# Eight heads at once in the top-16 look-up of a two-block model: bf16 look-up, pair sums for four heads, and gate groups behind 50 units

## What is computed

```python
q = (xt @ wq).reshape(T, PEER_HEADS, 2, PEER_DQ_HALF)
s1 = jnp.einsum('thd,nd->thn', q[:, :, 0], k1)      # 8 heads, 128 sub-keys
s2 = jnp.einsum('thd,nd->thn', q[:, :, 1], k2)
v1, i1 = lax.top_k(s1, 16)
v2, i2 = lax.top_k(s2, 16)
cand = (v1[..., :, None] + v2[..., None, :]).reshape(T, 8, 256)
cidx = (i1[..., :, None] * 128 + i2[..., None, :]).reshape(T, 8, 256)
sc, pos = lax.top_k(cand, 16)
eidx = jnp.take_along_axis(cidx, pos, axis=-1)
gate = jax.nn.softmax(sc, axis=-1)
# per token: sum over its 128 experts e of gate_e * gelu(x . u_e) * v_e
```

## Time and profile before

| | us |
|---|---|
| median of 3 runs | 3374.56 (3369.22 to 3378.02) |
| the profiled execution, its own time | 3360.43 |
| span of its trace | 3358.7 |
| PE busy | 3090.0 (92%) |
| DVE busy | 2289.5 (68%) |
| ACT busy | 1543.4 (46%) |
| mean granted TensorE clock | 0.957 |

### The profile page before, as it was taken

How to read it: one execution, slowest core, us unless ns; L and a number is a source line. 1 busy time by engine, 2 the same in 40 slices (tenths; PEclk the granted TensorE clock), 3 DMA queues, 4 the chain that set the end, 5 groups by cost and what they waited for, 6 DMA issues and landing times.

```text
span 3358.7 us, 59174 instructions
## 1 busy us (share of the span) xinstructions
PE 3090.0 (92%) x20832; PEld 2821.1 (84%) x20832; DVE 2289.5 (68%) x4056; ACT 1543.4 (46%) x2322; POOL 145.0 (4%) x135
## 2 busy tenths in 40 slices
PE   7988889999888897879999999998879999999997
PEld 7987879899867797779989988887779989988886
DVE  4547545555574555657998977777657998977776
ACT  4445244444452443534445545554534545545553
POOL 0001300000013000100000000000100000000000
PEclk9989789999897898999999999999999999999999
DMA  6544035555340454345765577776345765567775
GB/s 200 184 134 154 19 104 184 175 167 184 126 137 1 145 184 156 126 138 173 216 203 172 166 226 241 240 241 198 126 138 175 216 203 170 166 220 242 241 240 168
DMA packets 213000, 579.44 MB, mean 173 GB/s; under 512 B 23728, under 2 KB 88528, under 8 KB 212352
## 3 DMA queue, kind: packets, MB, share of 16 engines
q1 hardware_dynamic: 209216, 562.62, 53.1%
q0 software_dynamic: 3648, 14.99, 1.3%
HBM read 541.34 MB, written 36.18 MB: 172 GB/s over the span
## 4 chain that ended last, share of the span: by engine, by line
PE 76%; DVE 17%; ACT 3%; issue 2%; DMA 1%; POOL 1%; SPq 0%; DVEq 0%; ACTq 0%; POOLq 0%
PE work L658 33%; PE acc L680 30%; DVE wsp L406 5%; PE work L733 4%; PE acc L1054 2%; PE work L900 2%; DVE xsp L1415 1%; DVE rows_sb L1842 1%; DVE topi L1841 1%; DVE topi L1844 1%; DMA back<-acts_dram 1%; DVE topv L1843 1%; ACT wsp L403 1%; PE work L756 1%; DVE posi L1841 0%
## 5 line engine op out<-in xcount | busy, mean ns | idle before, releaser
L406 DVE TENSOR_TENSOR wsp<-ring,wsp 128x1024 fp32r<-128x1024 f32 x944 | 1157.7, 1227 | 641.8 <-ACT wsp L403 636.7
L658 PE MATMUL work<-xsp,wsp 128*128 128x256 f32 x12096 | 1512.8, 286 | 38.9 <-DVE wsp L406 31.6
L658 PEld LDWEIGHTS work<-xsp,wsp 128*128 128x128 f32 x12096 | 1483.8, 193 | 56.6 <-DVE wsp L406 32.7
L403 ACT ACTIVATE wsp<-ring 128x1024 fp32r<-128x1024 f32 x944 | 993.5, 1053 | 616.5 <-PE work L658 222.5
L680 PE MATMUL acc<-wsp,hsp 128*128 128x512 f32 x4128 | 954.4, 390 | 9.2 <-issue 7.2
L680 PEld LDWEIGHTS acc<-wsp,hsp 128*128 128x128 f32 x4128 | 770.3, 188 | 167.1 <-issue 10.4
L1357 ACT ACTIVATE hsp<-arena 128x256 fp32r (+1 forms) x256 | 107.1, 418 | 354.9 <-PE acc L680 335.5
L733 PE MATMUL work<-wsp,xsp 128*128 128x512 f32 x768 | 186.9, 403 | 35.1 <-DVE wsp L406 10.7
L733 PEld LDWEIGHTS work<-wsp,xsp 128*128 128x128 f32 x768 | 147.5, 195 | 73.0 <-DVE wsp L406 13.7
L1959 DVE TENSOR_TENSOR hsp<-arena,hsp 128x256 fp32r<-128x256 f32 x256 | 109.0, 426 | 56.9 <-ACT hsp L1357 56.6
L1930 DVE TENSOR_TENSOR one_hots<-one_hots,selT 128x512 bf16<-128x512 bf16 x384 | 139.5, 419 | 0.0
(11 more groups left out here) (299 smaller groups left out, 1903.9 us busy)
## 6 DMA issues: line engine op xcount, KB each, us to landing
ring<-in_stream SPq DMA_DIRECT2D x944, 512.0 KB, 3.5
back<-acts_dram SPq DMA_DIRECT2D x252, 128.0 KB, 3.2
acts_dram<-arena SPq DMA_DIRECT2D x168, 128.0 KB, 3.5
acts_dram<-acts SPq DMA_DIRECT2D x84, 128.0 KB, 3.6
rows_sb<-in_rows POOLq DMA_DIRECT2D x10, 512.0 KB, 5.0
h_saved_dram<-h POOLq DMA_DIRECT2D x2, 1024.0 KB, 4.2
h<-h_saved_dram POOLq DMA_DIRECT2D x2, 1024.0 KB, 6.5
scratch<-in_levels POOLq DMA_DIRECT2D x3, 448.0 KB, 4.7
```

The source lines that it names most:

```text
L403: self.eng.activation(dst[:, 0, :], src, ACT.Copy).then_inc(high_done, 1)
L406: self.eng.tensor_tensor(dst[:, 1, :], src, dst[:, 0, :].bitcast(F32), ALU.subtract)\
L658: mm = pe.matmul(out_, lhsT=w[:, a, 128 * c:128 * c + 128], rhs=xsp[:, b, c, :], start=(c == 0 and n == 0), stop=(c == DC - 1 and n == 2))
```

## The change

In the selection:

- **Pair sums** for four heads come from one instruction of 1024 elements in place of four of 256. A block is now two halves of four heads: eight `top16` over 128 scores, one pair sum, four `top16` over 256 sums.
- **Lows**: a `top16` over 256 sums has two lows, one in its middle and one at its end. One over 128 scores keeps its one. A block has 32 in the top-16 part (before: 24).
- **Look-up**: for each half m of the position (2 per block) one is_equal and one mult in bf16 over 2048 elements, and one reduce over the same 2048, in place of 8 triples of 256 f32 elements. Two lows stand behind each: 4 per block (before: 16). `topi` is cast to bf16 twice over (each index in two neighbouring places, `topf2`), `pfa` and `pfb` are bf16; the tile of the hits has the pair of neighbouring positions as its innermost dimension.
- Block total: 36 lows (before: 40). With three ahead the two blocks reach unit 74.

And `U_FIRST` is 78 (before: 84): the transposes and the first gate groups stand six units earlier, the 64 groups are spread over 48 units (before: 42), behind the last 50 units; ACT's and SP's rounds of 12 cover 72 units, so that both Exp now stand behind the Gelu of unit 71 and ahead of high 75, and six units follow one by one.

```diff
-U_FIRST = 84
+U_FIRST = 78
...
-            def top16(vals, idx, src, tmp):
+            def top16(vals, idx, src, tmp, lows):
                 step(dve.max(vals[:, 0:8], src))
                 step(dve.max_index(idx[:, 0:8], vals[:, 0:8], src))
                 step(dve.match_replace(tmp, vals[:, 0:8], src, LOWEST))
+                if lows == 2:
+                    split.upto(split.next)
                 step(dve.max(vals[:, 8:16], tmp))
                 step(dve.max_index(idx[:, 8:16], vals[:, 8:16], tmp))
                 split.upto(split.next)
...
                 for b in range(NB):
-                    for i in range(PH):
-                        for m in range(2):
...
-                            top16(topv[:, 2 * i + m, :], topi[:, 2 * i + m, :], src, cand[:, 0:128])
-                        c3 = cand.rearrange("p (a c) -> p a c", a=TOPK)
-                        step(tt(c3, topv[:, 2 * i, :].unsqueeze(2).broadcast_to([P, TOPK, TOPK]),
-                                topv[:, 2 * i + 1, :].unsqueeze(1).broadcast_to([P, TOPK, TOPK]), ALU.add))
-                        top16(selv[:, b, 2, 16 * i:16 * i + 16], posi[:, i, :], cand, cand2)
+                    for half in range(2):
+                        heads = range(PH // 2 * half, PH // 2 * (half + 1))
+                        for i in heads:
+                            for m in range(2):
...
+                                top16(topv[:, 2 * i + m, :], topi[:, 2 * i + m, :], src, cand2[:, 0:128], 1)
+                        pairs = topv[:, PH * half:PH * (half + 1), :].rearrange("p (h m) k -> p h m k", m=2)
+                        step(tt(cand.rearrange("p h (a c) -> p h a c", a=TOPK),
+                                pairs[:, :, 0, :].unsqueeze(3).broadcast_to([P, PH // 2, TOPK, TOPK]),
+                                pairs[:, :, 1, :].unsqueeze(2).broadcast_to([P, PH // 2, TOPK, TOPK]), ALU.add))
+                        for i in heads:
+                            top16(selv[:, b, 2, 16 * i:16 * i + 16], posi[:, i, :], cand[:, i % (PH // 2), :], cand2, 2)
...
-                    step(dve.tensor_copy(topf, topi))
+                    step(dve.tensor_copy(topf2, topi.unsqueeze(3).broadcast_to([P, 2 * PH, TOPK, 2])))
...
-                    for i in range(PH):
-                        for m, place in ((0, pfa), (1, pfb)):
-                            step(tt(c3, place[:, i, :].unsqueeze(2).broadcast_to([P, TOPK, TOPK]), io16, ALU.is_equal))
-                            step(tt(c3, c3, topf[:, 2 * i + m, :].unsqueeze(1).broadcast_to([P, TOPK, TOPK]), ALU.mult))
-                            step(dve.tensor_reduce(selv[:, b, m, 16 * i:16 * i + 16], c3, AX_X, ALU.add))
-                            split.upto(split.next)
+                    for m, place in ((0, pfa), (1, pfb)):
+                        at_k = place.rearrange("p h (k r) -> p (h k) r", r=2).unsqueeze(2).broadcast_to([P, PH * TOPK // 2, TOPK, 2])
+                        step(tt(hits.rearrange("p (k c r) -> p k c r", c=TOPK, r=2), at_k,
+                                iota2[:, 0:TOPK, :].unsqueeze(1).broadcast_to([P, PH * TOPK // 2, TOPK, 2]), ALU.is_equal))
+                        h3 = hits.rearrange("p (h k c) -> p h k c", h=PH, k=TOPK // 2)
+                        step(tt(h3, h3, topf2.rearrange("p (h m) c r -> p h m (c r)", m=2)[:, :, m, :].unsqueeze(2)
+                                .broadcast_to([P, PH, TOPK // 2, 2 * TOPK]), ALU.mult))
+                        step(dve.tensor_reduce(selv[:, b, m, :].rearrange("p (k r) -> p k r", r=2),
+                                               hits.rearrange("p (k c r) -> p k r c", c=TOPK, r=2), AX_X, ALU.add))
+                        split.upto(split.next)
+                        split.upto(split.next)
```

More of the change, by code:

```diff
@@ L139, in build_program @@
         selT = at("selT", place + 8192 + 4 * 1280, [P, 5, T], BF16)
+        hits = at("hits", place + 8192 + 4 * 768, [P, 2048], BF16)
+        topf2 = at("topf2", place + 8192 + 4 * 1792, [P, 2 * PH, TOPK, 2], BF16)
         cst = at("cst", place + 16384, [P, C_N])
@@ L148, in build_program @@
         topi = at("topi", place + 1024, [P, 2 * PH, TOPK], U32)
-        topf = at("topf", place + 2048, [P, 2 * PH, TOPK])
         posi = at("posi", place + 3072, [P, PH, TOPK], U32)
         posa = at("posa", place + 3584, [P, PH, TOPK], U32)
-        pfa = at("pfa", place + 4096, [P, PH, TOPK])
-        pfb = at("pfb", place + 4608, [P, PH, TOPK])
+        pfa = at("pfa", place + 4096, [P, PH, TOPK], BF16)
+        pfb = at("pfb", place + 4608, [P, PH, TOPK], BF16)
         place += 5120
@@ L285, in build_program @@
         selv = rows[:, 0:3 * 2 * HK].rearrange("p (b s k) -> p b s k", b=NB, s=3)
-        cand = rows[:, 768:1024]
-        cand2 = rows[:, 1024:1280]
+        cand = rows[:, 768:1792].rearrange("p (h n) -> p h n", h=PH // 2)
+        cand2 = rows[:, 1792:2048]
         rest = rows[:, 1920:2048]
@@ L1854, in peer @@
                 for b in range(NB):
-                    for i in range(PH):
-                        for m in range(2):
-                            c = 128 * m
-                            src = ACC[i // 2][:, 256 * (i % 2) + c:256 * (i % 2) + c + 128] if b == 0 \
-                                else sc1[:, 256 * i + c:256 * i + c + 128]
-                            top16(topv[:, 2 * i + m, :], topi[:, 2 * i + m, :], src, cand[:, 0:128])
-                        c3 = cand.rearrange("p (a c) -> p a c", a=TOPK)
-                        step(tt(c3, topv[:, 2 * i, :].unsqueeze(2).broadcast_to([P, TOPK, TOPK]),
-                                topv[:, 2 * i + 1, :].unsqueeze(1).broadcast_to([P, TOPK, TOPK]), ALU.add))
-                        top16(selv[:, b, 2, 16 * i:16 * i + 16], posi[:, i, :], cand, cand2)
+                    for half in range(2):
+                        heads = range(PH // 2 * half, PH // 2 * (half + 1))
+                        for i in heads:
+                            for m in range(2):
+                                c = 128 * m
+                                src = ACC[i // 2][:, 256 * (i % 2) + c:256 * (i % 2) + c + 128] if b == 0 \
+                                    else sc1[:, 256 * i + c:256 * i + c + 128]
+                                top16(topv[:, 2 * i + m, :], topi[:, 2 * i + m, :], src, cand2[:, 0:128], 1)
[5 more added lines that the diff above has]
+                            top16(selv[:, b, 2, 16 * i:16 * i + 16], posi[:, i, :], cand[:, i % (PH // 2), :], cand2, 2)
                     if b == 0:
                         dve.memset(st[:, 31:32], 0.0).then_inc(acc_free, 1)
-                    step(dve.tensor_copy(topf, topi))
+                    step(dve.tensor_copy(topf2, topi.unsqueeze(3).broadcast_to([P, 2 * PH, TOPK, 2])))
                     step(ts(posa, posi, 4, None, ALU.logical_shift_right))
@@ L1872, in peer @@
                     step(dve.tensor_copy(pfb, posi))
-                    io16 = iota[:, 0:TOPK].unsqueeze(1).broadcast_to([P, TOPK, TOPK])
-                    c3 = cand.rearrange("p (a c) -> p a c", a=TOPK)
-                    for i in range(PH):
-                        for m, place in ((0, pfa), (1, pfb)):
-                            step(tt(c3, place[:, i, :].unsqueeze(2).broadcast_to([P, TOPK, TOPK]), io16, ALU.is_equal))
-                            step(tt(c3, c3, topf[:, 2 * i + m, :].unsqueeze(1).broadcast_to([P, TOPK, TOPK]), ALU.mult))
-                            step(dve.tensor_reduce(selv[:, b, m, 16 * i:16 * i + 16], c3, AX_X, ALU.add))
-                            split.upto(split.next)
+                    for m, place in ((0, pfa), (1, pfb)):
[9 more added lines that the diff above has]
+                        split.upto(split.next)
                     g3 = selv[:, b, 2, :].rearrange("p (h k) -> p h k", h=PH)
```

## The result

| | us |
|---|---|
| median after, 5 runs | 3336.18 (3331.64 to 3339.03) |
| median before, 5 runs | 3374.56 (3369.22 to 3378.02) |
| ratio | 0.9889, 95% interval 0.9874 to 0.9903 |
| profiled execution after, its time and span | 3336.05, 3334.3 |

The forecast was 3335.5 within 3315 to 3357. In a later comparison, again with the kernel before beside it, the changed kernel had 3335.89 and a ratio of 0.9882 (0.9858 to 0.9906).

What follows compares the result with a forecast made beforehand. PE was taken as the bound, except DVE's work between lows in the top-16 part. Per layer 13.5 + 6.2 - 0.2 = 19.5 us, 39 in all, off the median 3374.6 gave 3335.5, range 3315 to 3357.

Steps and rivals of the forecast that it cites:

- Selection: Top-16 parts and look-ups: PE's losses to DVE fall from 19.5 to 6.0 us, 13.5 us gained per layer.
- the ledger: Running lag of lows in the selection: grows when low starts are over 2.88 us apart; PE loses what exceeds 3.3.
- The slack of 3.3 us: A low may lag 5.76 - 1.16 - 1.27 = 3.3 us behind its earliest place before PE waits.
- Look-up instructions: DVE's look-up: is_equal and mult in bf16 at 1.23 us, reduce over 2048 elements at 2.3 us.
- Passage: From selection to gate groups: 7.7 us lost before, 1.5 still taken for DVE's chain, 6.2 us gained per layer.
- Gate stage: Six units move into it at 2.92 instead of 2.88 us, costing 0.2 us per layer; it stays PE's.
- The ring: Loads sent behind lows: 2.8 us left after low and landing, highs delayed by 0.5 at most, priced at nothing.
- (a): Rival: one kind of look-up instruction runs at half the rate taken, 17 to 18 us more, 3353 us; chance 0.11.
- (b): Rival: the look-up's reduce runs at two per cycle, losses per layer 1.7 instead of 6.0, 3327 us; chance 0.07.
- (c): Rival: selection stays as slow through late ring loads, only the passage gains, 12 us, 3362 us; chance 0.05.
- (d): Rival: both look-up instruction kinds at half rate, clock falls in each look-up, 5.9 us per layer slower, 3386; chance 0.03.
- (e): Rival: lows don't get ahead since ACT or DVE wait elsewhere; left inside the range, no chance of its own.

Runs made afterwards that it cites:

- a split pair: Changed kernel with the two lows of each look-up half apart, one behind the mult and one behind the reduce: stage 419.8 us per layer, 3330.7 us.
- the f32 look-up: Changed kernel with the f32 triples of the kernel before, one low behind every fourth: stage 446.4 and 446.7 us, 3384.2 us in all.

## Why the prediction was right

By its own steps, per layer:

- **Price of a unit, 2.88 us:** measured 2.88 over 82 units without a gap.
- **Selection, 19.5 lost before, 6.0 forecast:** unit 0 to the transposes takes 231.27 us, 6.6 more than 78 x 2.88. Gained 12.9, forecast 13.5. The five gaps came where the ledger put them, with 1.5, 1.3, 0.6, 1.5, 1.4 for 1.3, 1.4, 0.6, 1.3, 1.4.
- **The slack of 3.3 us** carried this: without the mult, with a split pair and with three lows per half the stage came within 0.1, 0.4 and 0.3 us of what it gives. Where the clock fell behind longer stops, the ledger alone was 3.4 to 3.7 us short (443 for 446.4, 439.8 for 443.5).
- **Look-up instructions:** 1.22 and 2.29 for 1.23 and 2.31. The bf16 reduce, which had no row and was taken at the rate of the f32 one, has no higher rate. The Trainium skill, page "VectorE: DVE Perf Modes", section on the perf-mode tier table, has it so; the trace agrees (2.29 us for 2048 elements).
- **Passage:** unit 80 starts 9.6 us after the transposes' start, where unit 86 started 16.3 after the end of unit 83 (16.1 and the 0.2 of its tail): gained 6.7, forecast 6.2. The forecast counted the transposes at 1.3, as they were at the slow clock; they take 0.57. DVE's chain to the first groups costs 9.6 - 0.57 - 5.76 - 1.4 = 1.9 beside 1.5. The second Exp was later than forecast, since PE's own gap had not been counted in: ACT's high for unit 75 starts 6.0 us after PE's end of unit 71 and not 4.8. The same gap moved unit 75 back, so that the low for it (1761.61) still lay 1.7 us ahead of its last moment, near the forecast's 1.3.
- **Gate stage:** from unit 86 to unit 127 it was 163.1, from unit 80 it is 180.5, 17.4 for six units: 0.1 more than in the selection, forecast 0.2.
- **The ring, priced at nothing:** in the look-up ACT does wait for landings, up to 4.0 us, but DVE comes to that low later still, and each of the five gaps has DVE's low as its releaser.
- **Sum:** 12.9 + 6.7 - 0.1 = 19.5, forecast 19.5; the two errors of half a microsecond cancel.

The step to the whole time was less safe than it looked. Against the profiled execution of before, 3360.4 - 39 = 3321.4, the profiled one of after (3336.05) is 15 us off; against the median it is 0.7 off. That it came so near has luck in it: in the later comparisons the difference of the medians was 8 and 10 us smaller and 2 and 5.5 us larger than what the stages gave (17.6 for 26.0, 42.0 for 52.4, 40.9 for 39.0, 57.9 for 52.4). What was forecast well is the stage. Seen from the other executions the profiled one of before was 6 to 21 us short outside the stage.

Of the rivals, (a), (b) and (c) are out by the durations and the single piece of 840 matmuls, and (e) by the five gaps, which stood where the counts of lows put them. (d) was priced wrongly where it counts the clock: 7.8 us per layer forecast for four stops, 3.5 measured with stops of 6.0 us, since half of the slow units are hidden by the next wait. With the measured price it would lose 23.6 + 3.5 = 27.1 against 19.5, less the passage's 6.7: about 1 us per layer slower, which isn't to be told from no change. By its stops alone (23.6) it would even have been faster by some 2.6.

## What to carry to other kernels

When one engine prepares each unit for another in between its own work, keep a ledger of how late each preparation is, against the slack that the buffers give: the consumer pays only what goes beyond it, and the lag that is handed from one stage to the next counts as much as the longest stretch. Look for the parts of the producer's work that have slack to spare, and move preparations from there to the parts that have none; here the f32 look-up had it, and the shorter bf16 look-up made the move cheap. Fewer large instructions take less time in all but lengthen the stretch without a preparation; put one between them, not behind them in pairs. A short wait for an activation at the wrong place of an in-order stream can cost more than its length if TensorE slows down behind it, so place it where its input is ready and its reader has units in front of it.

## What the runs showed of the hardware

- The same program, profiled twice, differed by 14.8 us outside the stage and by 0.2 inside. The granted clock from 300 to 400 us was 0.78 in one and 0.80 in the other, 0.74 in the changed kernel's, and the longer of the two had the higher clock there, so this stretch doesn't explain it; which steps carry the difference stays open.
- After stops of 4.9 to 6.0 us PE began its next units at a granted clock of 0.50; after stops of up to 1.5 us (changed kernel) it stayed at 1.00. In the f32 look-up a unit behind a bracket of 1.85 took 4.26 us, with the clock falling to 0.50 while it ran, and the next one behind a bracket of 2.37 took 3.14 at 1.00. So a single stop's length doesn't tell it alone.
- Slow units just ahead of a wait for DVE cost nothing: with the reduce three times the second gap of a look-up was 3.88 us where the first was 5.99, and in the f32 look-up PE's starts stayed 6.6 us apart.
